# Two transformer blocks in fp32 on one core: a new order for the seven products of the second MLP matrix, with the embedding parts, the row transposes and a bank moved with it

## The chip, the cores and the metric

The kernel is one program on one core of a Trainium2 chip. The metric is device time in microseconds (us) of one execution, taken as the median of several. Shown here are three executions and, apart from them, one execution recorded by the hardware profiler.

The engines are TensorE (PE: matmuls and transposes), VectorE (DVE), ScalarE (ACT), GpSimd (POOL) and SyncE (SP, which here only issues transfers). Each works through its own list of instructions in order; an instruction that needs another engine's result waits on a semaphore, and everything behind it on its engine waits too.

## The reference, cut to what matters

512 tokens of width 1024 pass through two blocks. `first_block` has an RWKV-7 time mix and differential attention, `second_block` a gated linear attention and a dilated attention. Behind the mixing, both blocks do the same three things, and the change lies there:

```
merged = g_a * (o_a @ w_proj_a) + g_b * (o_b @ w_proj_b)
x = x + merged @ w_out                                    # the out projection ("wo")
h = rmsnorm(x)
x = x + square(relu(h @ w_ff1)) @ w_ff2                   # the MLP: 1024 -> 4096 -> 1024
gate = sigmoid(rmsnorm(x) @ w_ple_gate)
x = x + (p @ w_ple) * gate                                # the embedding part: p is 512 x 256
```

`second_block` spells them `w_mlp1`, `w_mlp2`, `w_pp` and `w_pg`, and ends in a last rmsnorm. Everything is fp32.

## The kernel before, in words

**Numbers.** A product of two fp32 matrices is made of three products of rounded parts: high by high, low by high and high by low. ACT makes the high part of a tile (a copy that rounds: `wh` of a weight, `SH`, `XH`, `YH`... of an activation), DVE the low part (tile minus high part: `wl`, `SL`, `XL`, `YL`...). A weight tile of 128 x 1024 is a unit; three slots each for `wh` and `wl` go round. In the trace all matmuls are line 131, transposes line 134, ACT operations mostly line 141, DVE's line 155 (two tensors) or 163 (with a scale). A matmul with 512 columns is the usual one.

**The MLP.** The 4096 hidden columns are worked through in four groups g of 1024. For each group the first matrix gives eight tiles `f1` (g, n), n = 0..7; ACT applies relu (tile T) and square (tile `hid`). The second matrix is multiplied with seven products in place of eight (Strassen's way, in Winograd's form): the group's activations and weights are cut into quarters, and some operands are sums of quarters. The activation sums are made on DVE, in place over `hid` and in a tile `E` (`dv_operands`: events ss 1 to 4). The weight sums are made on DVE in the four quarter tiles RB 11, 12, 21, 22 (`dv_weight_sums`: ts 1 to 4), which SP loads anew for each group (`sp_second`), each load waiting until the last low part was taken from the tile. Each product i (`product`) needs `SH` and `SL` of its operand (two slots) and two weight units, has 24 matmuls in two PSUM banks, and DVE then adds the two banks into `xt` with the reciprocal norm (`dv_mlp`).

**Who stands between.** In groups 0 to 2 the products alternate with the f1 tiles of the next group: f1(g+1, 0), product 0, f1(g+1, 1), product 1, and so on. In the last group there are no further f1 tiles. The embedding product `p @ w_ple` (two parts of 24 matmuls, `ple`) stands between the products there. The `prows` tile holds p by rows; PE transposes it (`pe_ple`, eight 128 x 128 transposes), and ACT and DVE split the result into `PPH` and `PPL`. As the last quarters of `xt` are complete, PE transposes them (`pe_turn`, in the order TURN, into banks 6 and 7), DVE adds them to XT (block 0), and the gate product begins on `YA`, `YB` (the first block's normed input, in halves), with its mean square taken by PE as ones x ACC.

**Order.** Each engine's instruction list comes out of a planner. The code of one kind of work on one engine is a lane; `arrange` plays all lanes against a clock of its own. On PE the lanes have fixed ranks, with the dense products (`pe_dense`) last but with patience before others come between. On DVE and ACT, lanes with no fixed slack (low parts, high parts, operands, weight sums) are ranked by when PE is to need them. So an edit in one lane moves others' instructions as well.

**Banks.** `self.ring` is the list of PSUM banks that the dense tiles take in turn (`take_bank`): (0, 1) in the MLP, (0, 1, 2) behind it.

Of the kernel before, what the change touches and what calls it, by code (L numbers as in the profile page):

```python
# [227 lines left out]
class Kernel:  # L228
# [273 lines left out]
    def pe_dense(self, s):  # L502
# [31 lines left out]
        for n in range(3, 8):  # L534
            yield from self.fm(s, "Y", ("pg", n))
        yield from self.fm_pair(s, "X2", ("ha",), ("gqk", 0, 0))
# [5 lines left out]
        yield from self.tm(s, "X2", ("gv", 0), [("xm", 0, 3, 7)])  # L542
# [24 lines left out]
    def dense_mlp(self, s, blk, merged, x):  # L567
# [1205 lines left out]
    def plan_ff(self, blk, w1, wp):  # L1773
        for j in range(4):
            self.plan("f1", w1, 0, 8, 256 * j, 256, "n", 2)
        made = ((11, "rb", 11), (21, "rb", 21), (11, "ts", 1), (11, "ts", 2), (22, "rb", 22), (12, "ts", 3), (21, "ts", 4))
# [5 lines left out]
        for g in range(3):  # L1782
            for n in range(8):
                if n % 2 == 0:
                    ci = self.chunk(w1, 0, 8, 1024 * (g + 1) + 128 * n, 256)
                self.piece(ci, "n", 2, n % 2)
                if n < 7:
                    product(g, n)
        for i in range(7):
            product(3, i)  # L1790
            if i == 2:
                ci = self.chunk(wp, 0, 2, 0, 1024)
            if i in (2, 5):
                self.piece(ci, "n", 2, i == 5)
# [78 lines left out]
    def mlp_tiles(self):  # L1873
# [21 lines left out]
        for blk in range(2):  # L1895
            for g in range(4):
# [13 lines left out]
    PRODUCTS = (("M1", (2, 3), True, 0, 0, 1), ("M2", (6, 7), True, 0, 0, 1), ("M5", (4, 5), True, 1, 1, 1), ("M6", (2, 3), False, 0, 1, -1),  # L1910
                ("M3", (4, 5), False, 0, 1, 1), ("M7", (2, 3), False, 1, 1, -1), ("M4", (2, 3), False, 1, 0, 1))
# [4 lines left out]
    def operand(self, g, i):  # L1916

        q = self.quarter
        return (q(g, 0, 0), q(g, 0, 1), self.E[:, :, :], q(g, 0, 0), q(g, 0, 1), q(g, 1, 0), q(g, 1, 1))[i]

    def operand_made(self, blk, g, i):
        tiles = {0: range(4), 1: range(4, 8), 6: range(4, 8)}.get(i)
        if tiles:
            return [self.at("hid", blk, g, n) for n in tiles]
        return [self.at("ss", blk, g, {2: 1, 3: 2, 4: 4, 5: 3}[i])]
# [11 lines left out]
    def dv_operands(self, s):  # L1937
        dv, at = self.dv, self.at
        for blk in range(2):
            for g in range(4):  # L1940
# [9 lines left out]
                self.splitting = x0 + 2  # L1950
# [7 lines left out]
                self.splitting = x0 + 3  # L1958
# [12 lines left out]
    def dv_weight_sums(self, s):  # L1971

        dv, at, RB = self.dv, self.at, self.RB
        for blk in range(2):
            for g in range(4):
                part = lambda q, h: RB[q][:, 2 * h:2 * h + 2, :]
                u = self.f2_units[blk, g]
                for k, q, a, b, i, lows, loads in ((1, 11, 11, 12, 2, 0, (11, 12)), (3, 12, 12, 22, 5, None, (22,)), (2, 11, 11, 22, 3, 2, ()), (4, 21, 11, 21, 6, 1, (21,))):
# [22 lines left out]
    def dv_mlp(self, s, blk):  # L2001
        dv = self.dv
        for (b, g, i), x in self.slot.items():
# [3 lines left out]
            for j in range(2):  # L2007
# [4 lines left out]
                if blk == 0 and g == 0 and i in (0, 2, 3, 6):  # L2012
# [30 lines left out]
    TURN = ((11, 1), (12, 4), (22, 5), (21, 6))  # L2043
    TURNED = (4, 5, 6, 7, 0, 1, 2, 3)

    def pe_turn(self, s, blk):
        pe = self.pe
        free = {p: ("f2e", blk, 3, 1, p) for p in range(2)}
        for q, i in self.TURN:
            th, nh = q // 10 - 1, q % 10 - 1  # L2050
            for p in range(2):
                yield
                pe.wait_ge(*[self.at("f2e", blk, 3, i, j) for j in range(2)], self.at(*free[p]))
# [5 lines left out]
                free[p] = ("fte", blk, q, p)  # L2059
# [13 lines left out]
    def ac_turn(self, s, gain):  # L2073
        ac = self.ac
        for q, i in self.TURN:
            th, nh = q // 10 - 1, q % 10 - 1
            for p in range(2):
                for f in range(2):
                    n = 4 * nh + 2 * p + f
                    yield  # L2080
                    ac.wait_ge(self.at("ft", 1, q, p), *([self.at("sl", 1, 3, 3), self.at("ss", 1, 3, 4)] if n < 4 else []))
                    ac.copy(self.YH[n][:, 256 * th:256 * th + 256], self.ps[6 + p][:, 256 * f:256 * f + 256], self.vec(gain, n)).then_inc(*s.up(("h", "Y2", n, th)))

    def dv_turn2(self, s, gain):
        dv = self.dv
        for q, i in self.TURN:
            th, nh = q // 10 - 1, q % 10 - 1
            for p in range(2):
                for f in range(2):
                    n, ts = 4 * nh + 2 * p + f, slice(256 * th, 256 * th + 256)  # L2090
                    yield
                    dv.wait_ge(self.at("h", "Y2", 4 * nh + 2 * p + 1, th), *([self.at("sl", 1, 3, 4)] if n < 4 else []))
# [3 lines left out]
    def ac_mlp3(self, s, gain):  # L2096
        ac = self.ac
        for n in self.TURNED:
            yield
            ac.wait_ge(self.at("xm", 0, 3, n))  # L2100
            ac.copy(self.YH[n], self.XT[:, n, :], self.vec(gain, n)).then_inc(*s.up(("h", "Y", n)))
            yield
# [4 lines left out]
    def dv_mlp3(self, s, gain):  # L2107
        dv = self.dv
        for n in self.TURNED:
# [3 lines left out]
            if n != 4:  # L2113
                yield
                dv.wait_ge(self.at("ysqd", n), s.now())
                dv.tensor_tensor(self.ACC[:, :], self.ACC[:, :], self.tile["ysq", n][:, :], ALU.add).then_inc(*s.up(("ysa", n)))
# [71 lines left out]
    def pe_norms(self, s):  # L2188
# [5 lines left out]
        yield from self.pe_mean_squares(s, "rst1", self.ACC, self.ps[4], ("ysa", 3), ("ysqd", 4), ("f2e", 0, 3, 4, 0))  # L2194
        yield from self.pe_spread(s, "rst1", self.T[2], self.ps[4], ("ms1",))
        yield from self.pe_mean_squares(s, "m1", self.ACC, self.ps[4], ("sqp", 7), ("rst1",))
        yield from self.pe_mean_squares(s, "m2", self.ACC2, self.ps[5], ("sqp2", 7), ("f2e", 0, 3, 4, 1))
# [732 lines left out]
    def pl_lnf(self, s):  # L2930
        pl = self.pl
        yield
        pl.wait_ge(self.at("sl", 1, 3, 2), self.at("ss", 1, 3, 2))
# [27 lines left out]
    SQUARED = [(0, 0), (1, 0), (0, 1), (1, 1), (2, 1), (3, 1), (2, 0), (3, 0)]  # L2961

    def ac_last_squares(self, s):
        ac = self.ac
        for x, (j, nh) in enumerate(self.SQUARED):
            sq = self.tile["lsq", x]
            yield
            ac.wait_ge(self.at("f2e", 1, 3, (1, 4, 5, 6)[x // 2], j % 2), *self.freed("lsq", x))
# [299 lines left out]
```

## Time and profile before

| | |
|---|---|
| median of three executions | 1932.8 us (1928.93, 1932.8, 1934.3) |
| profiled execution, own time | 1934.82 us |
| its span, first to last instruction | 1933.0 us |
| mean granted clock of TensorE | 0.989 of full |
| busy time of PE, DVE | 1883.5 us (97%), 1151.1 us (60%) |
| busy time of ACT, POOL | 855.3 us (44%), 98.8 us (5%) |
| chain of work that ended last, by engine | PE 87%, DVE 7%, ACT 2%, DMA 2%, issue 2% |

The last row follows the work back from the last instruction, at each step to what released it. A busy share says how much of the span an engine had work, not whether anyone waited for it. The granted clock is the share of full TensorE speed (2.4 GHz) that was granted; 0.50 is the lower level of 1.2 GHz.

### The profile page before, as it was taken

What the parts mean: (1) busy time and instruction counts of PE and PEld (TensorE: products, weight loads), DVE (VectorE), ACT (ScalarE), POOL (GpSimd) and SP (SyncE); (2) the same over time, 40 slices, a digit from 0 to 9 for tenths busy, and PEclk for the clock granted to TensorE, in tenths of its full rate; (3) what the DMA queues carried; (4) which work ended last, traced back from release to release, by engine and by line L of the source; (5) the groups of instructions that cost most, each with busy time, mean ns of one, the idle gap of its engine ahead of it and who ended that gap; (6) DMA issues with size and microseconds to landing.
All of it is one profiled execution on the core that took longest, in us unless ns stands there. A gap on an engine that the chain in (4) does not pass through costs nothing.

```text
span 1933.0 us, 23466 instructions
## 1 busy us (share of the span) xinstructions
PE 1883.5 (97%) x9426; PEld 1551.5 (80%) x9426; DVE 1151.1 (60%) x1777; ACT 855.3 (44%) x1318; POOL 98.8 (5%) x153
## 2 busy tenths in 40 slices
PE   7999999998999999899999999999999999999897
PEld 5887778877788888778888888898887888888786
DVE  5769665446456857788734335424345456857775
ACT  6435554323344444456634324333233444445363
POOL 2110111002000000000100000000000000000000
PEclk9999999999999999899999999999999999999999
DMA  6233211129423232212431222232255223232211
GB/s 226 66 91 119 85 55 40 45 78 328 127 66 110 87 131 87 87 44 79 142 117 47 88 69 85 92 105 82 93 196 185 87 66 122 81 124 89 97 44 65
DMA packets 158175, 194.65 MB, mean 101 GB/s; under 512 B 14826, under 2 KB 118932, under 8 KB 158067
## 3 DMA queue, kind: packets, MB, share of 16 engines
q1 hardware_dynamic: 151954, 181.91, 29.2%
q0 software_dynamic: 4528, 8.94, 1.4%
q10 hardware_dynamic: 1584, 2.30, 0.3%
q8 instruction: 75, 1.23, 0.3%
q14 instruction: 34, 0.27, 0.0%
HBM read 179.41 MB, written 15.54 MB: 101 GB/s over the span
## 4 chain that ended last, share of the span: by engine, by line
PE 87%; DVE 7%; ACT 2%; DMA 2%; issue 2%; POOL 0%; POOLq 0%; DVEq 0%; SPq 0%; ACTq 0%
PE bank L131 84%; PE bank L134 3%; DVE wl L155 1%; DMA prows<-in_p_dram 1%; ACT L141 1%; ACT wh L141 1%; DVE ACC L155 1%; DVE T L155 1%; DVE RB L155 0%; DMA scr_x<-XT 0%; DVE XL L163 0%; DVE XT L155 0%; ACT GP L141 0%; DVE ML L155 0%; DVE xt L163 0%
## 5 line engine op out<-in xcount | busy, mean ns | idle before, releaser
L131 PE MATMUL bank<-XH,wh 128*128 128x512 f32 (+1 forms) x1272 | 504.1, 396 | 5.3 <-DVE XL L163 2.2
L131 PE MATMUL bank<-XL,wh 128*128 128x512 f32 (+1 forms) x1272 | 497.0, 391 | 1.0 <-DVE XL L163 1.0
L141 ACT ACTIVATE wh<-raw 128x1024 fp32r<-128x1024 f32 (+1 forms) x239 | 252.8, 1058 | 534.2 <-PE bank L131 526.2
L155 DVE TENSOR_TENSOR wl<-raw,wh 128x1024 fp32r<-128x1024 f32 x238 | 292.8, 1231 | 269.6 <-ACT wh L141 269.1
L131 PE MATMUL bank<-XH,wl 128*128 128x512 f32 x1264 | 318.7, 394 | 0.0
L131 PEld LDWEIGHTS bank<-XH,wh 128*128 128x128 f32 (+1 forms) x1272 | 238.8, 188 | 60.5 <-issue 2.6
L131 PEld LDWEIGHTS bank<-XL,wh 128*128 128x128 f32 (+1 forms) x1272 | 238.9, 188 | 51.0 <-DVE XL L163 2.4
L131 PEld LDWEIGHTS bank<-XH,wl 128*128 128x128 f32 x1264 | 236.3, 189 | 49.6 <-issue 0.6
L141 ACT ACTIVATE wh<-RB 128x1024 fp32r<-128x1024 f32 x112 | 119.1, 1063 | 158.6 <-PE bank L131 158.6
L155 DVE TENSOR_TENSOR wl<-RB,wh 128x1024 fp32r<-128x1024 f32 x112 | 137.0, 1223 | 76.5 <-ACT wh L141 76.4
L131 PE MATMUL bank<-wh,SL 128*128 128x512 f32 x448 | 140.2, 395 | 12.6 <-DVE SL L155 12.6
L131 PE MATMUL bank<-wh,SH 128*128 128x512 f32 x448 | 139.6, 393 | 0.0
L131 PE MATMUL bank<-wl,SH 128*128 128x512 f32 x448 | 139.3, 392 | 0.0
L131 PEld LDWEIGHTS bank<-wh,SL 128*128 128x128 f32 x448 | 85.2, 191 | 31.1 <-DVE SL L155 13.5
L131 PEld LDWEIGHTS bank<-wl,SH 128*128 128x128 f32 x448 | 85.2, 190 | 18.0
L131 PEld LDWEIGHTS bank<-wh,SH 128*128 128x128 f32 x448 | 84.6, 190 | 17.6
L163 DVE SCALAR_TENSOR_TENSOR xt<-bank,scales,xt 128x512 f32<-128x512 f32 x104 | 77.7, 747 | 4.1 <-DVE xt L163 0.9
L155 DVE TENSOR_TENSOR RB<-RB,RB 128x1024 f32<-128x1024 f32 x64 | 78.2, 1221 | 1.4
L155 DVE TENSOR_TENSOR T<-bank,RST 128x512 f32<-128x512 f32 x58 | 40.0, 689 | 60.6 <-PE bank L131 60.3
L131 PE MATMUL bank<-wh,XH 128*128 128x512 f32 x192 | 60.4, 396 | 0.0
L131 PE MATMUL bank<-wh,XL 128*128 128x512 f32 x192 | 59.7, 392 | 0.0
L131 PE MATMUL bank<-wl,XH 128*128 128x512 f32 x192 | 59.7, 392 | 0.0
(446 smaller groups left out, 2583.7 us busy)
## 6 DMA issues: line engine op xcount, KB each, us to landing
raw<-in_w_in_dram SPq DMA_DIRECT2D x58, 1024.0 KB, 5.2
RB<-in_w_ff_dram SPq DMA_DIRECT2D x16, 1024.0 KB, 5.0
raw<-in_w_ff_dram SPq DMA_DIRECT2D x16, 1024.0 KB, 5.3
RB<-in_w_mlp_dram SPq DMA_DIRECT2D x16, 1024.0 KB, 5.1
raw<-in_w_mlp_dram SPq DMA_DIRECT2D x16, 1024.0 KB, 5.3
raw<-in_w_out_dram SPq DMA_DIRECT2D x8, 1024.0 KB, 5.2
scr_x<-XT POOLq DMA_DIRECT2D x16, 256.0 KB, 4.6
XT<-scr_x SPq DMA_DIRECT2D x8, 512.0 KB, 10.9
```

The source lines that it names most:

```text
L131: return self.put(ns, lambda e: e.matmul(out, lhsT, rhs, start=start, stop=stop, skip_group_check=True))
L134: return self.put(109, lambda e: e.transpose(out, in_, ident))
L141: return self.put(ns, lambda e: e.activation(out, in_, func, bias=bias, scale=scale), func)
L155: return self.put(self.ns(out), lambda e: e.tensor_tensor(out, a, b, op))
L163: return self.put(self.ns(out), lambda e: e.scalar_tensor_tensor(out, a, s, b, op0, op1))
```

## The change

- **Order of the products.** Before: M1, M2, M5, M6, M3, M7, M4. After: M1, M5, M6, M3, M7, M2, M4. The bank pairs follow: (2, 3) and (4, 5) in turn, where M2 had (6, 7). The operand sums, the weight sums, the loads of the quarters and the transposes of finished quarters follow that order; the last weight sum goes into RB 12.
- **Embedding parts.** In the last group the two `ple` parts stand ahead of product 0 and of product 1. Before, they stood behind product 2 and behind product 5.
- **Row transposes.** `pe_ple` additionally waits for the last tile of the out projection.
- **Bank.** In block 0 the ring has a fourth bank (3) from the MLP to the start of the second block's projections.
- **Squares.** For the gate's norm in block 0 the squares on ACT come behind each four copies, and DVE's additions into ACC behind each four low parts.

```diff
-    PRODUCTS = (("M1", (2, 3), True, 0, 0, 1), ("M2", (6, 7), True, 0, 0, 1), ("M5", (4, 5), True, 1, 1, 1), ("M6", (2, 3), False, 0, 1, -1),
-                ("M3", (4, 5), False, 0, 1, 1), ("M7", (2, 3), False, 1, 1, -1), ("M4", (2, 3), False, 1, 0, 1))
+    PRODUCTS = (("M1", (2, 3), True, 0, 0, 1), ("M5", (4, 5), True, 1, 1, 1), ("M6", (2, 3), False, 0, 1, -1), ("M3", (4, 5), False, 0, 1, 1),
+                ("M7", (2, 3), False, 1, 1, -1), ("M2", (4, 5), True, 0, 0, 1), ("M4", (2, 3), False, 1, 0, 1))
...
         for i in range(7):
+            if i < 2:
+                yield from self.ple(s, blk, i)
             yield from self.product(s, blk, 3, i)
-            if i in (2, 5):
-                yield from self.ple(s, blk, i == 5)
-        self.ring, self.last_use[2] = (0, 1, 2), self.pair_after[2]
+        self.ring, self.last_use[2], self.last_use[3] = (0, 1, 2) if blk else (0, 1, 2, 3), self.pair_after[2], self.pair_after[3]
...
-        made = ((11, "rb", 11), (21, "rb", 21), (11, "ts", 1), (11, "ts", 2), (22, "rb", 22), (12, "ts", 3), (21, "ts", 4))
+        made = ((11, "rb", 11), (11, "ts", 1), (11, "ts", 2), (22, "rb", 22), (12, "ts", 3), (21, "rb", 21), (12, "ts", 4))
...
-                yield
-                low(1)
-                yield
-                self.splitting = x0 + 4
-                dv.wait_ge(s.now(), at("sh", blk, g, 1))
-                dv.tensor_tensor(q(g, 0, 1), q(g, 0, 1), q(g, 0, 0), ALU.add).then_inc(*s.up(("ss", blk, g, 4)))
-                for i in range(2, 7):
+                for i in range(1, 7):
                     yield
                     low(i)
+                    if i == 2:
+                        yield
+                        self.splitting = x0 + 3
+                        dv.wait_ge(s.now(), at("sh", blk, g, 2))
+                        dv.tensor_tensor(q(g, 0, 0), q(g, 0, 1), q(g, 0, 0), ALU.add).then_inc(*s.up(("ss", blk, g, 4)))
...
-                for q in (11, 22, 12, 21):
+                for q in (22, 11, 21, 12):
                     yield
                     if g:
                         u = self.f2_units[blk, g - 1]
-                        sp.wait_ge(at("lo", u[{11: 3, 22: 4, 12: 5, 21: 6}[q]][1]), *{11: [at("ts", blk, g - 1, 4, 1)], 22: [at("ts", blk, g - 1, 2, 1)], 12: [], 21: []}[q])
+                        sp.wait_ge(at("lo", u[{11: 2, 22: 3, 12: 6, 21: 5}[q]][1]), *{11: [at("ts", blk, g - 1, 4, 1)], 22: [at("ts", blk, g - 1, 3, 1)], 12: [], 21: [at("ts", blk, g - 1, 4, 1)]}[q])
...
-    TURN = ((11, 1), (12, 4), (22, 5), (21, 6))
+    TURN = ((12, 3), (22, 4), (11, 5), (21, 6))
...
-            pe.wait_ge(self.at("prw", blk))
+            pe.wait_ge(self.at("prw", blk), self.at("acc", "wo", blk, 7))
```

The rows below are the instruction lists as the two programs have them, buffer numbers included. The first place is PE in block 0's out projection (`MH`, `ML`: high and low part of the merged rows). Before:

```order
L131 MATMUL bank<-MH_203,wl_77 128x512 x6
L131 MATMUL bank<-MH_203,wl_75 128x512 x6
L134 MATMUL bank<-ident_49,prows_226 128x128 x8
L131 MATMUL bank<-MH_203,wh_74 128x512
L131 MATMUL bank<-ML_204,wh_74 128x512
```

After, at the end of the projection, where the first f1 tile (`XH`, `XL`) follows:

```order
L131 MATMUL bank<-MH_203,wh_72 128x512
L131 MATMUL bank<-ML_204,wh_72 128x512
L131 MATMUL bank<-MH_203,wl_75 128x512 x8
L134 MATMUL bank<-ident_49,prows_226 128x128 x8
L131 MATMUL bank<-XH_67,wh_73 128x512
L131 MATMUL bank<-XL_68,wh_73 128x512
```

The eight transposes move from the middle of the projection's eight tiles to behind the last one. The second place is DVE at the last group of block 0, from the moment at which `hid` is complete. Before:

```order
L155 TENSOR_TENSOR E_216<-hid_206 128x1024
L155 TENSOR_TENSOR hid_206<-hid_206 128x4x256
L155 TENSOR_TENSOR wl_75<-RB_214,wh_72 128x1024
L163 SCALAR_TENSOR_TENSOR xt_207<-bank,scales_228,xt_207 128x512
L155 TENSOR_TENSOR wl_76<-RB_212,wh_73 128x1024
L163 SCALAR_TENSOR_TENSOR xt_207<-bank,scales_228,xt_207 128x512
L155 TENSOR_TENSOR RB_212<-RB_212,RB_215 128x1024
L155 TENSOR_TENSOR hid_206<-E_216,hid_206 128x4x256
L155 TENSOR_TENSOR SL_210<-hid_206,SH_208 128x1024
```

After:

```order
L155 TENSOR_TENSOR E_216<-hid_206 128x1024
L155 TENSOR_TENSOR hid_206<-hid_206 128x4x256
L155 TENSOR_TENSOR hid_206<-E_216,hid_206 128x4x256
L155 TENSOR_TENSOR wl_75<-raw_71,wh_72 128x1024
L155 TENSOR_TENSOR SL_210<-E_216,SH_208 128x1024
L155 TENSOR_TENSOR wl_76<-RB_212,wh_73 128x1024
```

The low part that product 1 needs stood ninth, and now stands fifth, and it is of `E`, no longer of a `hid` quarter. The third place is PE at the end of block 0's MLP, where the last products (`wl_75` by `SH`), the last quarter's transposes and the gate product (`YA`, `YB`) meet. Before:

```order
L131 MATMUL bank<-wl_75,SH_209 128x512 x2
L134 MATMUL bank<-ident_49,xt_207 128x128 x8
L131 MATMUL bank<-YA_217,wh_73 128x512
...
L131 MATMUL bank<-YA_217,wl_75 128x512 x4
L131 MATMUL bank<-ones_52,ACC_61 128x1 x4
L131 MATMUL bank<-YB_219,wh_73 128x512
```

After:

```order
L131 MATMUL bank<-YA_217,wl_76 128x512 x4
L134 MATMUL bank<-ident_49,xt_207 128x128 x8
L131 MATMUL bank<-YA_217,wh_74 128x512
...
L131 MATMUL bank<-YA_217,wl_75 128x512 x4
L131 MATMUL bank<-YB_219,wh_73 128x512
...
L131 MATMUL bank<-YB_219,wl_75 128x512 x4
L131 MATMUL bank<-ones_52,ACC_61 128x1 x4
```

Before, the transposes stood ahead of the gate product and the mean square (ones x ACC) behind 36 matmuls of it. Now the transposes stand behind the first 12 matmuls, and the mean square behind 72. The transposes that spread its result over the tokens follow 12 matmuls later before, and 16 matmuls later now.

## Rows read from the trace of the kernel before

**Rows 1.** Waits of PE by what ended them: total, times, longest
```profile
PE bank L131 <- DVE SL L155: 12.6, 2, 6.3
PE bank L134 <- DMA prows<-in_p_dram: 8.2, 2, 5.3
PE bank L131 <- DVE XT L155: 1.6, 2, 0.8
```

**Rows 2.** PE's timeline, row transposes of block 0: start, duration, instruction, [idle before]
```profile
472.13 1.97 PE L134 MATMUL bank<-ident,prows 128*128 128x128 f32 x8 [5.31 <-DMA prows<-in_p_dram]
473.75 0.78 PE L131 MATMUL bank<-MH,wh 128*128 128x512 f32 x1
...
477.31 0.40 PE L131 MATMUL bank<-MH,wh 128*128 128x512 f32 x1
```

**Rows 3.** PE's timeline, row transposes of block 1
```profile
1484.33 1.97 PE L134 MATMUL bank<-ident,prows 128*128 128x128 f32 x8 [2.92 <-DMA prows<-in_p_dram]
1485.95 0.78 PE L131 MATMUL bank<-OGH,wh 128*128 128x512 f32 x1
...
1488.20 0.39 PE L131 MATMUL bank<-OGH,wh 128*128 128x512 f32 x1
```

**Rows 4.** PE's timeline, end of block 0's out projection
```profile
510.93 1.98 PE L131 MATMUL bank<-MH,wl 128*128 128x512 f32 x8
513.68 0.50 PE L131 MATMUL bank<-XH,wh 128*128 128x512 f32 x1 [0.78 <-DVE XT L155]
```

**Rows 5.** PE's timeline, last group: product 1 of block 0, then of block 1
```profile
816.03 1.22 PE L131 MATMUL bank<-wh,SL 128*128 128x512 f32 x2 [6.32 <-DVE SL L155]
...
822.12 0.62 PE L131 MATMUL bank<-wl,SH 128*128 128x512 f32 x2
...
1829.02 1.22 PE L131 MATMUL bank<-wh,SL 128*128 128x512 f32 x2 [6.32 <-DVE SL L155]
...
1832.51 0.63 PE L131 MATMUL bank<-wl,SH 128*128 128x512 f32 x2
```

**Rows 6.** Stretches: length, busy time of PE, PEld, DVE, ACT, POOL, granted clock, DMA share, GB/s
```profile
472.13:477.31 5.18, 5.18 (x17) 4.41 (x17) 2.07 (x4) 1.81 (x3) 0.00 (x0) 0.50 1.04 372
803.66:867.74 64.08, 56.09 (x250) 45.42 (x248) 54.34 (x58) 33.77 (x41) 0.00 (x0) 0.92 0.08 25
1816.65:1879.47 62.82, 56.23 (x256) 45.84 (x254) 52.16 (x59) 38.55 (x62) 0.55 (x1) 0.95 0.10 33
882.49:921.35 38.86, 38.56 (x170) 30.39 (x168) 36.30 (x57) 26.71 (x42) 1.05 (x2) 1.00 0.36 109
```

**Rows 7.** DVE's timeline, last group of block 0
```profile
806.51 1.22 DVE L155 TENSOR_TENSOR E<-hid 128x1024 f32<-128x1024 f32 x1
...
814.76 1.22 DVE L155 TENSOR_TENSOR SL<-hid,SH 128x1024 fp32r<-128x1024 f32 x1
```

**Rows 8.** PE's timeline, last quarter's transposes, block 0 and block 1
```profile
866.92 1.06 PE L134 MATMUL bank<-ident,xt 128*128 128x128 f32 x8 [1.67 <-DVE xt L163]
867.74 2.09 PE L131 MATMUL bank<-YA,wh 128*128 128x512 f32 x8
...
1878.57 1.06 PE L134 MATMUL bank<-ident,xt 128*128 128x128 f32 x8 [0.27 <-DVE xt L163]
```

**Rows 9.** PE's, then DVE's timeline, norm of block 0's gate and its first eviction
```profile
876.30 1.05 PE L131 MATMUL bank<-ones,ACC 128*128 128x1 f32 x8
...
882.49 0.69 DVE L155 TENSOR_TENSOR T<-bank,RST 128x512 f32<-128x512 f32 x1
```

**Rows 10.** DVE's, then PE's timeline, start of the second block's projections
```profile
920.60 0.75 DVE L163 SCALAR_TENSOR_TENSOR XL<-XT,gg,XH 128x512 fp32r<-128x512 f32 x1 [0.79 <-ACT XH L141]
...
921.41 0.44 PE L131 MATMUL bank<-XL,wh 128*48 128x512 f32 x1 [0.36 <-DVE XL L163]
```

**Rows 11.** SP's, then ACT's timeline: load of a chunk of the first MLP matrix, first use
```profile
751.90 0.37 SPq L119 DMA_DIRECT2D raw<-in_w_ff_dram  x1
...
782.10 1.06 ACT L141 ACTIVATE wh<-raw 128x1024 fp32r<-128x1024 f32 x1 [3.43 <-PE bank L131]
```

More of the change, by code:

```diff
@@ L541, in pe_dense @@
                         yield from self.fm(s, "X2", ("gqk", c, 2 * pr + i))
-        yield from self.tm(s, "X2", ("gv", 0), [("xm", 0, 3, 7)])
+        yield from self.tm(s, "X2", ("gv", 0), self.last_use[3])
         yield from self.tm(s, "X2", ("gv", 1), [("free", "gv", 0, 3)])
@@ L1788, in plan_ff @@
                     product(g, n)
+        ci = self.chunk(wp, 0, 2, 0, 1024)
         for i in range(7):
+            if i < 2:
+                self.piece(ci, "n", 2, i)
             product(3, i)
[L1791 to L1794, printed above, removed]
     def sp_spill1(self, s):
@@ L1918, in operand @@
         q = self.quarter
-        return (q(g, 0, 0), q(g, 0, 1), self.E[:, :, :], q(g, 0, 0), q(g, 0, 1), q(g, 1, 0), q(g, 1, 1))[i]
+        return (q(g, 0, 0), self.E[:, :, :], q(g, 0, 0), q(g, 0, 0), q(g, 1, 0), q(g, 0, 1), q(g, 1, 1))[i]
     def operand_made(self, blk, g, i):
-        tiles = {0: range(4), 1: range(4, 8), 6: range(4, 8)}.get(i)
+        tiles = {0: range(4), 5: range(4, 8), 6: range(4, 8)}.get(i)
         if tiles:
             return [self.at("hid", blk, g, n) for n in tiles]
-        return [self.at("ss", blk, g, {2: 1, 3: 2, 4: 4, 5: 3}[i])]
+        return [self.at("ss", blk, g, {1: 1, 2: 2, 3: 4, 4: 3}[i])]
     def ac_operands(self, s):
@@ L1977, in dv_weight_sums @@
                 u = self.f2_units[blk, g]
-                for k, q, a, b, i, lows, loads in ((1, 11, 11, 12, 2, 0, (11, 12)), (3, 12, 12, 22, 5, None, (22,)), (2, 11, 11, 22, 3, 2, ()), (4, 21, 11, 21, 6, 1, (21,))):
+                for k, q, a, b, i, lows, loads in ((1, 11, 11, 12, 1, 0, (11, 12)), (2, 11, 11, 22, 2, 1, (22,)), (3, 12, 12, 22, 4, None, ()), (4, 12, 11, 21, 6, 4, (21,))):
                     for h in range(2):
@@ L2011, in dv_mlp @@
                 dv.wait_ge(self.at("f2", blk, g, i, j), self.at("irst", blk))
-                if blk == 0 and g == 0 and i in (0, 2, 3, 6):
+                if blk == 0 and g == 0 and i in (0, 1, 2, 6):
                     dv.tensor_scalar(acc, self.ps[pair[j]][:, :], by, ALU.mult).then_inc(*s.up(("f2e", blk, g, i, j)))
@@ L2047, in pe_turn @@
         pe = self.pe
-        free = {p: ("f2e", blk, 3, 1, p) for p in range(2)}
+        free = {p: self.FF_FREE[blk] for p in range(2)}
         for q, i in self.TURN:
@@ L2052, in pe_turn @@
                 yield
-                pe.wait_ge(*[self.at("f2e", blk, 3, i, j) for j in range(2)], self.at(*free[p]))
+                pe.wait_ge(*[self.at("f2e", blk, 3, i, j) for j in range(2)], *[self.at(*e) for e in free[p]])
                 for f in range(2):
@@ L2058, in pe_turn @@
                 t.then_inc(*s.up(("ft", blk, q, p)))
-                free[p] = ("fte", blk, q, p)
+                free[p] = [("fte", blk, q, p)]
     def dv_turn(self, s):
@@ L2101, in ac_mlp3, with ac_squares @@
             ac.copy(self.YH[n], self.XT[:, n, :], self.vec(gain, n)).then_inc(*s.up(("h", "Y", n)))
+            if n in (7, 3):
+                yield from self.ac_squares(s, n - 3)
+    def ac_squares(self, s, n0):
+        ac = self.ac
+        for n in range(n0, n0 + 4):
             yield
@@ L2112, in dv_mlp3 @@
             dv.scalar_tensor_tensor(self.YL[n], self.XT[:, n, :], self.vec(gain, n), self.YH[n].bitcast(F32), ALU.mult, ALU.subtract).then_inc(*s.up(("l", "Y", n)))
-            if n != 4:
+            for m in {7: (5, 6, 7), 3: (0, 1, 2, 3)}.get(n, ()):
                 yield
-                dv.wait_ge(self.at("ysqd", n), s.now())
-                dv.tensor_tensor(self.ACC[:, :], self.ACC[:, :], self.tile["ysq", n][:, :], ALU.add).then_inc(*s.up(("ysa", n)))
+                dv.wait_ge(self.at("ysqd", m), s.now(), *([self.at("ysqd", 4)] if m == 5 else []))
+                dv.tensor_tensor(self.ACC[:, :], self.ACC[:, :], self.tile["ysq", m][:, :], ALU.add).then_inc(*s.up(("ysa", m)))
     def pl_ple(self, s, blk, p):
@@ L2193, in pe_norms @@
         yield from self.pe_turn(s, 0)
[L2194 removed]
+        yield from self.pe_mean_squares(s, "rst1", self.ACC, self.ps[4], ("ysa", 3), ("ysqd", 4), ("f2e", 0, 3, 5, 0))
         yield from self.pe_spread(s, "rst1", self.T[2], self.ps[4], ("ms1",))
         yield from self.pe_mean_squares(s, "m1", self.ACC, self.ps[4], ("sqp", 7), ("rst1",))
[L2197 removed]
+        yield from self.pe_mean_squares(s, "m2", self.ACC2, self.ps[5], ("sqp2", 7), ("f2e", 0, 3, 5, 1))
         yield from self.pe_spread(s, "rstB", self.T[2], self.ps[4], ("m1",))
```

17 lines of the change are left out of this document (9 added, 8 removed).

## The prediction

> **What bounds the kernel now.** PE does: it is busy 97% of the span and holds 87% of the chain that ended last, so a gain can only come out of its remaining idle time or out of stretches in which it runs at a lower clock. I therefore read the list of PE's waits first. It has two large entries beyond the start-up, and both are at places that the change touches: the low part `SL`, twice, 12.6 us together, and the rows of p, twice, 8.2 us together [rows 1]. Then I read PE's timeline around each, because a long wait has a second price. Behind the 5.31 us wait for `prows` the granted clock is 0.50, the lower level of 1.2 GHz, until 477.31 [rows 2, 6], and the same shape stands behind each `SL` wait. Full speed is 0.227 us for a 512-column matmul: eight have a record of 1.98 us, which is seven steps and a last 0.39 [rows 4]. In the slow stretches one step is about 0.43. Between the end of one matmul's slot and the next start there is 0.16 us more than the idle figure, since the record of the last one runs on (513.68 less 510.93 and eight steps is 0.94, the row says 0.78) [rows 4].
>
> **Part 1, row transposes.** Block 0: the wait is 5.31 + 0.16 = 5.47 us, the eight transposes take 473.75 - 472.13 = 1.62, and the eight matmuls up to 477.31 take 3.56 where 8 x 0.227 = 1.81 would do [rows 2]. Together 5.47 + 1.62 + 1.75 = 8.8. Block 1: 2.92 + 0.16, 1.62, and six matmuls up to 1488.20 in 2.25 instead of 1.36 [rows 3]: 3.1 + 1.6 + 0.9 = 5.6. In the new place the load has had some 35 us more, so nothing waits for it. The transposes themselves are not removed. But there PE already stands idle for 0.94 us, for the first normed tile [rows 4] (in block 1 too: two waits, 1.6 us together [rows 1]), and eight transposes at full clock take 867.74 - 866.92 = 0.82 us [rows 8]. They fit, so I charge 0.1 per block: **8.7 + 5.5 gained**. If that cover were gone, they would cost 0.8 each. `PPH` and `PPL` are made later, but the first user is the last group, hundreds of us on.
>
> The Trainium skill (TensorE: Matmul & The Clock Gate, Part 4: PE-mode transpose) gives about 275 ns for one such transpose inside a kernel. Eight one after the other would be 2.2 us by that, an estimate, and would overrun the gap by 1.3 us per block, 2.6 in all. The row's spacing of 0.10 us each speaks against it here, and the sum goes by the row.
>
> **Part 2, the last group.** Before, product 1 (M2) follows product 0 at once and needs hidden tiles that were just made. `E` starts at 806.51, when the last `hid` is there, and DVE then has three weight low parts, two evictions and a weight sum ahead of the `SL` at 814.76 [rows 7]. PE waits 6.32 + 0.16 = 6.48 us. The following 14 matmuls, up to 822.12, take 6.09 instead of 3.18, so 2.91 more. In block 1 the wait is the same 6.48, and eight slow matmuls take 3.49 instead of 1.81, 1.68 more [rows 5]. The last quarter's transposes wait 1.67 + 0.16 = 1.83 and 0.27 + 0.16 = 0.43 us for `xt` [rows 8]. At stake are 6.48 + 2.91 + 1.83 = **11.2** in block 0 and 6.48 + 1.68 + 0.43 = **8.6** in block 1.
>
> After, embedding part 0, product 0 and embedding part 1 stand between the last f1 tile and product 1. Each is 24 matmuls, 5.44 us, so product 1 begins at 803.66 + 16.3 = 820.0 in the old trace's time. The `SL` that it needs is that of `E`, now the fifth instruction after `hid` is complete: 806.51 + 5 x 1.22 = 812.6 at the latest. It has 7 us to spare, and this wait goes away. What is left is DVE's volume. In the 64.08 us from 803.66 to the gate product DVE is busy 54.34 us [rows 6]. Take out 11.2 and 52.9 us are left for the same work: DVE is 1.4 us over. What is late then is the last eviction into `xt`. Although the transposes that need it now stand 12 matmuls (2.7 us) into the gate product, I place 1.4 us there and 0.3 at quarter 11, whose product comes just before. In block 1, 62.82 - 8.6 = 54.2 us stand against 52.16 of DVE work [rows 6]. It fits on average, but DVE's evictions and the low parts of the next operand `YA`/`YL` bunch at the end; I take 1.3, a little less than in block 0, with 0 and 3 as ends. Gain: 11.2 - 1.7 = **9.5**, and 8.6 - 1.3 = **7.3**.
>
> **Part 3, the gate of block 0.** The mean square stands 36 matmuls later on PE and its spread 4 more: 40 x 0.227 = 9.1 us. The first eviction was 882.49 - 867.74 = 14.75 us after the gate product's start Y0 [rows 8, 9]. One weight low part (1.1 us) stood just before it and need not now, so it comes at 14.75 + 9.1 = 23.8 or 22.7; I take 23.2. The gate product has a fourth bank, so PE can run on meanwhile. But DVE's evictions, additions and low parts start later as well, and at their end the second block's projections wait for the last `XL`. From the first eviction to the end of that `XL` (920.60 + 0.75) are 38.86 us, of which DVE is busy 36.30 [rows 6, 10]. Two weight low parts (2.3 us) move ahead of it, and 34.0 to 36.6 are left; with a backlog the idle part shrinks, so I take 34.5. The last `XL` is then there at Y0 + 57.7. PE waited only 0.36 for it [rows 10], so it was due at Y0 + 53.3, and at 54.1 with the last quarter's transposes now inside. That makes a wait of 3.6, less the old 0.36: **3.2 lost**. Ends: 0, if the evictions start at 22.7 and the idle is gone and ACT's hand-offs shrink too; 8, with 23.8 + 36.6 (a wait of 6.3) and the lower clock behind it, which was worth 1.7 to 2.9 above. The bank itself brings nothing by itself, as PE has no wait for a bank in that stretch.
>
> **Part 4, the steady groups.** In groups 0 to 2 an f1 tile (5.44 us) stands between any two products, so the slack of product 1's operand is that of the new last group, 7 us. No PE wait of these groups is in the list before, so there is nothing to gain. I charge nothing; the cover is the f1 tiles.
>
> **Sum.** 8.7 + 5.5 + 9.5 + 7.3 - 3.2 = 27.8. Span 1933.0 becomes 1905.2, the execution's own time 1934.8 becomes 1907.0. That execution was 2.0 above the median of 1932.8, so the median becomes 1905.0.
>
> **Rivals.** *A, nothing given back:* all 34.0 us at stake (8.7 + 5.5 + 11.2 + 8.6) arrive and the gate costs nothing. For it: ACT and DVE are played against one clock by the planner, which may move YL work out of the way. Against it: DVE at 1.4 over. Time 1932.8 - 34.0 = 1898.8. *B, DVE becomes the bound of the last groups and the gate:* the gate wait is 8, and each last group gives back 3 more. Gain 27.8 - 4.8 - 6 = 17, time 1915.8. For it: 54.34 us of work in 52.9. *C, only the row transposes pay:* the `SL` wait turns into one of like size later in the group, for an operand sum or a weight sum. Gain 14.2 - 3.2 = 11, time 1921.8. Against it: the 7 us of slack. *D, slower:* in the six steady groups the operand of product 1 comes late, because `hid`'s three sums now stand in front of weight low parts and evictions that PE needs sooner. Each miss would be priced like the old one, up to 6.5 us plus 2.9 of clock, six times 56 us: 1961. It decides once a group loses 27.8 / 6 = 4.6 us, which needs the operand some 11 us later than I place it. The same rival could come from SP. The reload of a quarter now waits for the last weight sum, in front of the next weight chunk in SP's list. But that chunk is issued at 751.90, lands in about 5 us and is first used at 782.10 [rows 11], so a delay under 25 us is free.
>
> **Chances.** Forecast (gain 23 to 31) 0.60, A 0.15, B 0.15, C 0.06, no net gain 0.02, D 0.02. A measurement tells a change of 0.3%, 5.8 us, from none: faster 0.96, same 0.02, slower 0.02. The forecast's own range is 1902 to 1910. The full range goes from A, less 2 for the spread of the runs, to B: 1897 to 1916. Outside it are C, D, no gain, and the edges of A and B, some 0.15.
>
> **What would show it.** In the new trace PE's list should have no `prows` and no `SL` entry, and the transposes of `prows` should stand at about 505 without a slow stretch behind them. There should be a wait for `xt` of about 1 to 2 us at the last quarter of each block, and one of 3 to 4 us for `XL` or `XH` at the start of the second block's projections. The stretch from the last f1 tile to the gate product should shrink from 64.1 to about 54.5. The prediction is wrong if a wait of over 3 us stands in a steady group, if the transposes cost 2 us at their new place, or if the gate's last `XL` is on time or over 6 us late.

## The result and the profile after

The changed kernel takes 1908.9 us in the median (1906.97 to 1911.25, four runs) against 1933.4 us for the kernel before (four executions, one more than in the table above). The ratio is 0.9878, with a 95% interval of 0.9859 to 0.9898: 24.5 us faster. Timed twice more beside the experiments it gave 1907.2 and 1907.1 us, where the kernel before gave 1932.0 and 1931.9: 24.8 us faster both times. The profiled execution has a span of 1905.0 us and took 1906.97 us itself. The forecast was a gain of 27.8 us, which made 1905 for the median and 1905.2 for the span. The span came out at that, the medians' gain is 3 us smaller.

The page's head, of the changed kernel:

```profile
span 1905.0 us, 23473 instructions
PE 1876.2 (98%) x9426; PEld 1547.3 (81%) x9426; DVE 1148.1 (60%) x1777; ACT 853.9 (45%) x1318; POOL 99.7 (5%) x153
```

PE's waits in it, by what ended them (total, times, longest):

```profile
PE bank L131 <- DVE XL L163: 4.1, 2, 2.2
...
PE bank L131 <- ACT XH L141: 1.4, 1, 1.4
PE bank L131 <- ACT T L141: 1.1, 4, 0.3
PE bank L134 <- DVE xt L163: 1.1, 1, 1.1
...
PE bank L134 <- DVE YA L163: 0.6, 1, 0.6
```

Both large entries of [rows 1] are gone, `SL` and `prows`. New are `XH`, a larger share for `XL`, two more waits for `T`, and one for `YA`. Next PE's timeline at the new place of the row transposes (two rows), in embedding part 0, at the last quarter's transposes of block 0, at the start of the second block's projections, and at the transposes of quarter 11 in block 1's last group:

```profile
500.29 1.06 PE L134 MATMUL bank<-ident,prows 128*128 128x128 f32 x8
501.11 0.47 PE L131 MATMUL bank<-XH,wh 128*128 128x512 f32 x1
...
794.70 0.50 PE L131 MATMUL bank<-PPH,wh 128*128 128x512 f32 x1 [0.28 <-ACT T L141]
...
849.92 1.07 PE L134 MATMUL bank<-ident,xt 128*128 128x128 f32 x8 [1.07 <-DVE xt L163]
...
902.01 0.43 PE L131 MATMUL bank<-XH,wh 128*48 128x512 f32 x1 [1.37 <-ACT XH L141]
904.38 0.43 PE L131 MATMUL bank<-XL,wh 128*48 128x512 f32 x1 [1.95 <-DVE XL L163]
...
1845.41 0.63 PE L134 MATMUL bank<-ident,xt 128*128 128x128 f32 x4 [0.60 <-DVE YA L163]
```

The transposes take 501.11 - 500.29 = 0.82 us, in the time in which PE stood idle before [rows 4]; the first f1 tile follows them with no wait. The wait for `xt` is 1.07 + 0.16 us (the 0.16 is the prediction's: the time that the record before a wait runs on). The two waits at the start of the projections are 1.37 + 1.95 + 0.32 = 3.64 us.

To see where the time went I cut PE's timeline at seven instructions that every version has, and took differences of their starts. They are the `X,UB` matmuls that wait for `X` (at about 258 us), the first wait for `T` in each block's f1 tiles, the end of the last f1 tile in each block, the `KI` transposes that PE waits for (about 957), and the first instruction behind the transposes of block 1's last quarter. All numbers are us.

| stretch | before | changed | difference | forecast |
|---|---|---|---|---|
| start to `X,UB` | 259.9 | 258.0 | -1.9 | none |
| to f1 of block 0: row transposes | 266.2 | 257.4 | -8.8 | -8.7 |
| f1 and the steady groups, block 0 | 277.6 | 277.6 | 0.0 | 0 |
| last group, gate, start of block 1 | 168.7 | 164.1 | -4.6 | -6.3 |
| to f1 of block 1: row transposes | 566.7 | 561.2 | -5.5 | -5.5 |
| f1 and the steady groups, block 1 | 277.6 | 277.6 | 0.0 | 0 |
| last group, block 1 | 62.8 | 55.5 | -7.2 | -7.3 |
| to the end | 53.6 | 53.6 | 0.0 | 0 |

Behind the start, two more executions of the changed kernel give the same stretches within 0.1 us, but for the second stretch of one of them (258.0). The first row is no effect of the change, as experiment 5 shows; without it the traces differ by 26.1 us. The kernel before has one trace only, so what chance did in it shows only where an experiment runs the same instructions again.

### The profile page after: what moved, and what is told of

Its sections match the earlier page's. It is cut to its first block, busy times and chain, and to the rows that moved or that the text cites. A ratio compares the mean times of both kernels' runs of the same rounds, so it can differ in the third digit from the quotient of the medians.

```text
span 1905.0 us, 23473 instructions
## 1 busy us (share of the span) xinstructions
PE 1876.2 (98%) x9426; PEld 1547.3 (81%) x9426; DVE 1148.1 (60%) x1777; ACT 853.9 (45%) x1318; POOL 99.7 (5%) x153
## 3 DMA queue, kind: packets, MB, share of 16 engines
q8 instruction: 75, 1.23, 0.3%
## 4 chain that ended last, share of the span: by engine, by line
PE 88%; DVE 7%; ACT 2%; issue 2%; DMA 1%; POOL 0%; POOLq 0%; DVEq 0%; ACTq 0%
PE bank L131 86%; PE bank L134 2%; DVE wl L155 2%; DVE xt L163 1%; ACT L141 1%; DVE XL L163 1%; DVE T L155 0%; DMA scr_x<-XT 0%; DVE XT L155 0%; DVE RB L155 0%; ACT wh L141 0%; DVE ACC L155 0%; ACT GP L141 0%; DVE SL L155 0%; DVE YA L163 0%
```

## The experiments

Below, *gate* is the fourth row of the table above (before 168.7, changed 164.1) and *last 1* its row for block 1's last group (62.8 and 55.5). Both are lengths in us.

**1. Row transposes back in the projection.**

```diff
-            pe.wait_ge(self.at("prw", blk), self.at("acc", "wo", blk, 7))
+            pe.wait_ge(self.at("prw", blk))
```

> The changed kernel with one part undone: the row transposes may go as soon as the rows of p have landed, so they stand in the middle of the out projection again. Theory of the sum (5.47 + 1.62 + 1.75 and 3.1 + 1.6 + 0.9 us, less the 0.94 us gap that they fill now): both waits for prows come back, 5.3 and 2.9 us, with the lower clock behind them, and the kernel is 14 us slower than the changed one, 10 faster than before. Rival: the transposes cost as much at their new place as they did at the old one (they delay the first f1 tile), so the difference is under 6 us.

1920.6 us, ratio 0.9943 (0.9928 to 0.9958): 11.7 to 13.5 slower than the changed kernel, by which of its medians is taken. PE's timeline of this version, both blocks:

```profile
468.51 1.97 PE L134 MATMUL bank<-ident,prows 128*128 128x128 f32 x8 [4.90 <-DMA prows<-in_p_dram]
...
1474.83 1.85 PE L134 MATMUL bank<-ident,prows 128*128 128x128 f32 x8 [2.78 <-DMA prows<-in_p_dram]
```

The two stretches are 264.7 and 566.6 us, 7.3 and 5.4 above the changed kernel's, 12.7 together where 14.3 separate the kernels at the top. The waits are shorter by 0.4 and 0.1 us here; the rest of the difference is in the slow matmuls behind, of which there are fewer in block 0. The rival, a cost at the new place, is out: all other stretches stay.

**2. Only the embedding parts first**, in the kernel before (`plan_ff` moved with it, as in the change):

```diff
         for i in range(7):
+            if i < 2:
+                yield from self.ple(s, blk, i)
             yield from self.product(s, blk, 3, i)
-            if i in (2, 5):
-                yield from self.ple(s, blk, i == 5)
```

> The kernel before with one part done: the embedding parts ahead of product 0 and product 1 in the last group, old order of the products. Theory 1, it is the two embedding parts (10.9 us of PE work) that give DVE the time: the SL of product 1 is there at about 804 of the changed kernel's time against 810 needed, no SL wait, and the kernel gains 15 to 18 us of its own, 1916. Rival, the new order of the products is what removes the wait, since M5 needs E where M2 needs a later low part: the wait for SL stays above 3 us in both blocks and the gain is under 10 us.

1921.2 us, ratio 0.9943 (0.9927 to 0.9960): 10.6 us faster than the kernel before, where 15 to 18 were expected. No wait for `SL` is left. Gate 162.5, last 1 56.3: 6.2 and 6.5 us gained. The mechanism is as theory 1 has it; its size was set too high, since I counted the 18 us at stake and not what is given back at the end of the group.

**3. The new order without the embedding parts in front**: the changed kernel with the same lines the other way round. The moved row transposes, the bank and the squares stay in.

> The changed kernel with one part undone: the embedding parts behind products 2 and 5 again, new order of the products. Theory 1 (see the run with the embedding parts alone): E is begun at the same moment, and the SL of product 1 stands tenth on DVE behind it, some 10 us, where product 0 covers 3; a wait of about 7 us comes back in both blocks with the lower clock behind it, and the kernel is 15 to 19 us slower than the changed one. Rival: the order alone shortens the chain to the SL, the wait is under 3.5 us and the clock stays up, 3 to 8 us slower.

1918.8 us, ratio 0.9931 (0.9917 to 0.9946), 10 to 12 slower than the changed kernel. PE's timeline, product 1 in both blocks:

```profile
807.65 1.22 PE L131 MATMUL bank<-wh,SL 128*128 128x512 f32 x2 [7.03 <-DVE SL L155]
...
1813.04 1.22 PE L131 MATMUL bank<-wh,SL 128*128 128x512 f32 x2 [7.03 <-DVE SL L155]
```

The wait is back at 7.03 us, longer than the old 6.32 [rows 5]. Last 1 is 64.2, worse than before by 1.4; gate is 166.6. The new order does not bring the low part any earlier by itself. Again the sum was put too high (15 to 19 expected), for the same reason. Against the kernel before, the order, the bank and the squares together gain 2.1 us in gate and lose 1.4 in last 1: 0.7 us in all without the embedding parts. The rest of this version's 13.0 us is the moved row transposes.

**4. Both parts that pay, alone**: the kernel before with the edits of 1 (forward) and 2, old order, three banks, squares one by one. Run twice, the second time beside the changed kernel.

> The kernel before with two parts done: embedding parts ahead of products 0 and 1, row transposes behind the projection; old order of the products, three banks, squares one by one. Theory 1, from the runs so far: these two parts hold the whole gain and the new order of the products adds nothing; adding up the stretches gives the changed kernel's time less 1.6 us at block 0's gate and plus 0.7 us in block 1's last group, so 1 us faster, and within 2.5 us of it in any case. Rival, the parts need each other (the order of the products pays only once the embedding parts stand first): 5 us or more slower than the changed kernel.

> The kernel before with embedding parts first and rows behind the projection alone, timed in five rounds beside the changed kernel. From the stretches of its first trace: 1.8 us (0.09%) faster than the changed kernel; by the medians the two can hardly be told apart, and neither is 3 us apart from the other. Rival: the old order of the products costs 3 us or more.

1905.8 us, ratio 0.9870 (0.9854 to 0.9887), then 1906.6 us, 0.9873 (0.9858 to 0.9888). Gate is 161.5 and 163.1, last 1 is 56.3 both times. So the whole of what is left out is worth 0.8 us in block 1's last group, and costs 1.0 to 2.6 in block 0. The version has two of the change's parts and is as fast as the whole of it; the medians can't tell them apart. PE's timeline of the first run, last quarter of block 0, then the second block's projections:

```profile
847.28 0.95 PE L134 MATMUL bank<-ident,xt 128*128 128x128 f32 x7 [1.32 <-DVE xt L163]
851.55 1.11 PE L131 MATMUL bank<-YA,wh 128*128 128x512 f32 x2 [2.05 <-DVE YA L163]
...
904.72 0.44 PE L131 MATMUL bank<-XL,wh 128*48 128x512 f32 x1 [0.35 <-DVE XL L163]
```

The 3.64 us wait is down to 0.35 + 0.16, and 3.7 us of waits stand at the gate product's start instead. The clock stays up behind the short wait at the projections, where the changed kernel loses 3.2 us to the lower one (worked out in part 3 below). The second run has the same waits within 0.02 us, and yet its gate is 1.5 us longer. The stretch behind the 2.05 us wait shows why, in the second run:

```profile
852.20:856.20 4.00, 3.59 (x8) 2.67 (x9) 3.69 (x7) 3.36 (x7) 0.00 (x0) 0.59 0.00 0
```

In the first run the clock of the same stretch (852.20 to 856.20) is 1.00.

**5. The changed kernel itself, again**, twice.

> The changed kernel itself, on the same chip as the three runs beside it: 1906 to 1911 us. Theory on the start: which of two courses the first 60 us take (a slow stretch behind the wait for LD at 37 to 38 us, or none) is settled anew in each execution, as the instruction lists there are the same in all kernels; so this execution may well have it, and would then end 1.5 to 2 us later than the first one profiled. Rival: the course belongs to the kernel, and it comes without the slow stretch again.

> The changed kernel itself, five rounds beside the run above: 1906 to 1909 us, a ratio of 0.987 to 0.988 to before. Every stretch behind the first 260 us as in the two traces of it so far, within 0.1 us; only the start differs, by up to 2.5 us.

1907.2 us, ratio 0.9875 (0.9861 to 0.9890), and 1907.1 us, 0.9871 (0.9857 to 0.9886). In the first of them `X,UB` starts at 259.4, in the second at 257.5, with the same lists. PE's timeline of the first, and stretches of it (length, busy times, granted clock third from the end):

```profile
37.91 0.47 PE L131 MATMUL bank<-LD,LS 128*128 128x512 f32 x1 [1.48 <-ACT LD L141]
```
```profile
36.00:38.00 2.00, 0.52 (x3) 0.12 (x2) 1.78 (x3) 1.93 (x4) 0.00 (x0) 1.00 0.00 0
38.00:40.00 2.00, 2.00 (x5) 1.01 (x6) 0.00 (x0) 1.99 (x4) 0.00 (x0) 0.92 0.00 0
40.00:42.00 2.00, 2.00 (x6) 1.52 (x6) 1.73 (x2) 2.00 (x4) 0.00 (x0) 0.50 0.01 4
```

The first execution of the changed kernel had 0.40 us at this place and a clock of 1.00 from 36 to 46 us. Its slow stretch came earlier. These are 8 to 24 us in the first execution of the changed kernel, then in this one:

```profile
8.00:24.00 16.00, 13.11 (x57) 10.77 (x57) 10.54 (x17) 13.02 (x22) 6.61 (x12) 0.89 0.83 244
```
```profile
8.00:24.00 16.00, 12.20 (x61) 9.26 (x59) 11.25 (x23) 13.47 (x23) 7.20 (x13) 1.00 0.83 248
```

The kernel before went the way of this one (1.00 from 8 to 24 us, 0.72 from 40 to 46). The course of the start belongs to the execution, and with it the 1.9 us of the first table.

**6. Squares one by one**, in the changed kernel:

```diff
             ac.copy(self.YH[n], self.XT[:, n, :], self.vec(gain, n)).then_inc(*s.up(("h", "Y", n)))
-            if n in (7, 3):
-                yield from self.ac_squares(s, n - 3)
+            yield
+            ac.wait_ge(self.at("imb", 0), *(self.freed("ysq", n) if n != 4 else []))
...
```

> The changed kernel with one part undone: squares and their additions follow each single tile, so the mean square stands behind 36 matmuls of the gate product again, and the last quarter's transposes stand ahead of it. Theory, the late mean square makes the 3.3 us wait at the second block's projections: that wait falls under 1 us, and a wait for xt of 1 to 3 us at the transposes remains or grows, since nothing of the gate product stands before them; 1 to 3 us faster than the changed kernel in all. Rival, DVE's volume makes the wait wherever the mean square stands: the 3.3 us stay within 0.7, and the kernel is no faster or up to 3 us slower.

1906.3 us, ratio 0.9868 (0.9854 to 0.9883); gate 163.7, 0.4 less. Both halves of the theory came about, and cancel. PE's timeline, and the clock behind the first of its rows:

```profile
849.93 1.07 PE L134 MATMUL bank<-ident,xt 128*128 128x128 f32 x8 [3.78 <-DVE xt L163]
...
905.64 0.43 PE L131 MATMUL bank<-XL,wh 128*48 128x512 f32 x1 [0.35 <-DVE XL L163]
```
```profile
850.75:854.75 4.00, 4.00 (x14) 3.14 (x13) 3.90 (x7) 2.67 (x5) 1.05 (x2) 0.57 0.00 0
```

The last `xt` comes at the same moment as in the changed kernel (849.93 and 849.92), whatever PE does meanwhile. The wait for it, 3.78 us, is longer than the 1 to 3 expected, and the lower clock stands behind it.

**7. Three banks for the gate**, in the changed kernel:

```diff
-        self.ring, self.last_use[2], self.last_use[3] = (0, 1, 2) if blk else (0, 1, 2, 3), self.pair_after[2], self.pair_after[3]
+        self.ring, self.last_use[2], self.last_use[3] = (0, 1, 2), self.pair_after[2], self.pair_after[3]
```

> The changed kernel with one part undone: three banks for the gate of block 0. With the first eviction at about 23 us after the gate product's start and 5.4 us of matmuls per tile, three banks are full after 16 us. Theory: PE then waits for a bank, 3 to 7 us, and about as much of the 3.3 us wait at the second block's projections goes away; 1 to 5 us slower in all. Rival, as the prediction has it: the bank brings nothing by itself, within 1 us.

1908.3 us, ratio 0.9883 (0.9866 to 0.9899); gate 164.7, 0.6 more. PE's timeline:

```profile
868.13 1.12 PE L134 MATMUL bank<-ident,T 128*128 128x128 f32 x4 [2.99 <-DVE T L166]
870.73 1.65 PE L131 MATMUL bank<-YB,wh 128*128 128x512 f32 x3 [1.48 <-DVE T L155]
...
907.93 0.43 PE L131 MATMUL bank<-XL,wh 128*48 128x512 f32 x1 [0.35 <-DVE XL L163]
```

The fourth bank moves a wait of 4.5 us from the gate to the end of the stretch and saves 0.6. Without it the part up to the `ones` x `ACC` matmuls of the projections (at 904.99 in the changed kernel) is 3.8 us longer, and the part behind them 3.2 us shorter, as the lower clock behind the projections' wait is gone. "Brings nothing by itself" was near in size, though for another reason than I gave: without it PE does wait.

**8. Product 0 ahead of both embedding parts**, in the changed kernel:

```diff
         for i in range(7):
-            if i < 2:
-                yield from self.ple(s, blk, i)
             yield from self.product(s, blk, 3, i)
+            if i == 0:
+                yield from self.ple(s, blk, 0)
+                yield from self.ple(s, blk, 1)
```

> The changed kernel with one place moved: product 0, then both embedding parts, then product 1. The 0.28 us wait for T in the second bank of embedding part 0 (0.44 with the tail, in both blocks) goes away, since product 0 stands between; the slack of product 1's SL is the same. Theory: 0.5 to 1 us faster by the stretch from the last f1 tile to the gate product, too little for the medians. Rival: product 0's own low part or weights come late without the embedding part in front, a wait of over 1 us for SL, wl or SH, and slower.

1907.1 us, ratio 0.9874 (0.9859 to 0.9889). The wait for `T` is gone and one of 0.34 us for `PLT` between the two parts stands in its place, so last 1 stays at 55.5. Neither theory had that one. Gate is 165.2, 1.1 more, and all of it lies behind the projections' last wait. From 904 to 916, in steps of 4 us, the clock is 0.57, 0.50 and 0.65 there, so the slow stretch is longer in this execution.

**9. Less work for DVE**, in the changed kernel. The six additions of the turned quarters 12, 22 and 11 to XT take 64 columns instead of 512, so this version leaves most of block 0's MLP result out:

```diff
-                dv.tensor_tensor(o, o, self.ps[6 + p][:, :].rearrange("p (f t) -> p f t", f=2), ALU.add).then_inc(
+                c = 256 if q == 21 else 32
+                dv.tensor_tensor(o[:, :, 0:c], o[:, :, 0:c], self.ps[6 + p][:, :].rearrange("p (f t) -> p f t", f=2)[:, :, 0:c], ALU.add).then_inc(
```

> The changed kernel with DVE's work at the end of block 0's last group cut: the six additions of the turned quarters 12, 22 and 11 to XT take 64 columns in place of 512, so most of the MLP's result stays out of XT in block 0. That frees some 3 us of DVE ahead of the last eviction into xt. Theory, DVE's volume sets the last quarter and the gate: the 1.07 us wait for xt goes, the mean square comes earlier, and the 3.3 us wait at the second block's projections shrinks by about the same 3 us; 3 to 6 us faster than the changed kernel, with the lower clock gone there as well. Rival, the waits come from PE's banks and the order, not from DVE's time: under 1 us faster.

1900.5 us, ratio 0.9841 (0.9824 to 0.9857), 6.6 us faster than the changed kernel; gate 156.4, that is 7.7 less. No wait for `xt` is left in block 0, and one wait at the projections:

```profile
899.78 0.43 PE L131 MATMUL bank<-XL,wh 128*48 128x512 f32 x1 [0.70 <-DVE XL L163]
```

About 3 us of DVE work taken away give back 7.7 us, more than the 3 to 6 expected. The traces add it up: the waits for `XT` and `xt` in the last group are gone (0.46 and 1.23 us), the wait at the projections is 0.86 in place of 3.64, and the same instructions from `ones` x `ACC` to the `KI` transposes take 3.2 us less, at full clock:

```profile
900.38:949.16 48.78, 47.35 (x224) 39.18 (x224) 40.64 (x61) 36.20 (x49) 7.43 (x11) 1.00 0.41 137
```

This is the clearest sign that DVE's volume sets block 0's last group and gate. The planner also moved the mean square forward here, from behind 72 matmuls of the gate product to behind 60, so part of it may be order; no run separates the two.

## Why the prediction held, step by step

**Part 1, row transposes: right to 0.1 us** (8.8 and 5.5 measured, 8.7 and 5.5 forecast). The price of such a wait is three things, and all three had to be counted: the wait, the transposes at the lower clock, and the slow matmuls behind. The transposes fit into the idle gap before the f1 tile. That it came to 0.1 us is partly luck, since the number of slow matmuls differs between executions: with the transposes at the old place the stretch was longer by 8.8, 8.3 and 7.3 us in block 0 (before, experiments 2 and 1) and by 5.5, 6.6 and 5.4 in block 1. The group of the last group's transposes in the kernel before, by line (busy, mean ns of one, idle before):

```profile
L134 PE MATMUL bank<-ident,xt 128*128 128x128 f32 x32 | 4.2, 275 | 1.7 <-DVE xt L163 1.7
```

One record is 275 ns long, which is what the Trainium skill states for a transpose within a kernel (TensorE: Matmul & The Clock Gate, Part 4: PE-mode transpose). But eight start 0.10 us apart and take 0.82 us, so the figure is the length of one and not the price of one more. The estimate of 2.2 us for eight, worked out from it, did not come.

**Part 2, the last groups: right in mechanism.** The `SL` of product 1 was ready 7 us early, as worked out. DVE's timeline of the changed kernel, with the `SL` at its end (needed by PE at 810.41):

```profile
796.67 1.22 DVE L155 TENSOR_TENSOR E<-hid 128x1024 f32<-128x1024 f32 x1
...
801.46 1.22 DVE L155 TENSOR_TENSOR SL<-E,SH 128x1024 fp32r<-128x1024 f32 x1
```

Block 1 gained 7.2 where 7.3 was forecast, but the last part of that sum is right by luck. I had given 1.3 us back at its end, where DVE's work bunches, and looked for a wait for `xt` at the last quarter. That wait did not come. One for `YA` at quarter 11, one quarter earlier (0.60 + 0.16), and the one for `T` named below (0.44) came in its place, and add up to 1.2. In block 0 the wait at the last quarter was 1.23 against 1.4, and one for `XT` at quarter 22 took 0.30 + 0.16. I missed a wait in both blocks, for `T` in the second bank of embedding part 0 (0.28 + 0.16): with two banks in the ring, the part that now follows f1 at once needs the bank that ACT is still emptying. And DVE's own timeline shows why the last `xt` is late:

```profile
844.15 1.41 DVE L163 SCALAR_TENSOR_TENSOR YA<-XT,pvt,YA 128x512 fp32r<-128x512 f32 x2
845.48 1.22 DVE L155 TENSOR_TENSOR wl<-raw,wh 128x1024 fp32r<-128x1024 f32 x1
846.62 0.75 DVE L163 SCALAR_TENSOR_TENSOR YA<-XT,pvt,YA 128x512 fp32r<-128x512 f32 x1
847.28 0.75 DVE L163 SCALAR_TENSOR_TENSOR xt<-bank,scales,xt 128x512 f32<-128x512 f32 x1
```

It is busy without a gap, with the gate product's low parts ahead of the eviction. DVE is busy 55.6 us of the 57.8 from the last f1 tile to the end of those transposes:

```profile
792.90:850.74 57.84, 56.20 (x261) 45.53 (x260) 55.64 (x60) 32.67 (x40) 0.00 (x0) 1.00 0.11 36
```

The prediction counted the embedding parts and the order as one thing. Experiments 2, 3 and 4 show that the embedding parts carry the gain, and that the new order has no share in it that a median could show.

**Part 3, the gate: right in place, its cost a quarter too low** (3.2 forecast, 4.4 measured). The first eviction came at 870.38, 24.5 us after the gate product's first matmul (845.92), where 23.2 was forecast, and the last `XL` ended 58.4 us after it (57.7). PE would have needed it 54.8 us after it (54.1), so both ends came 0.7 us later than placed and their difference, the wait, was 3.64 us (3.6). Its size is right in part by luck. The mis-sized term is the clock behind this wait, which I had put into the range's end and not into the value. Here are the 8 us from 902.75, with most of the second wait in them:

```profile
902.75:906.75 4.00, 2.20 (x10) 1.88 (x10) 2.78 (x4) 1.40 (x2) 0.00 (x0) 0.79 0.46 121
906.75:910.75 4.00, 4.00 (x15) 3.52 (x15) 2.04 (x5) 0.00 (x0) 1.63 (x2) 0.50 0.41 143
```

The lower clock holds for some 7 us, in the kernel before for some 3.5. These are the same instructions in both, from `ones` x `ACC` to the `KI` transposes, before and changed:

```profile
922.01:972.40 50.39, 48.95 (x223) 40.35 (x223) 40.65 (x61) 36.24 (x49) 7.46 (x11) 0.97 0.37 123
```
```profile
904.99:957.00 52.01, 50.57 (x223) 41.94 (x224) 40.73 (x61) 36.20 (x49) 7.43 (x11) 0.93 0.40 132
```

At full clock they take 48.8 us (experiments 2, 4, 7 and 9). So the clock cost 3.2 us in the changed kernel, in all three of its traces, and 1.6 in the trace before: 1.6 more. Block 0's part as a whole gained 4.6 and not 6.3. Of the missing 1.7, some 0.5 lies in the last group (`T` and `XT`) and 1.2 in the gate: the 1.6 of clock, less 0.4 gained elsewhere in it.

**Part 4, the steady groups: right.** 277.6 us before and after, in both blocks, in every version.

**Rivals.** A (all 34.0 us) is out by the waits at the last quarter and the gate; B has the right mechanism, a DVE that is busy nearly throughout, but of its 10.8 us beyond the forecast only 1.7 came; C and D did not occur. The medians moved by 24.5 to 24.8 and not by 26.1. The start can make that difference, and so can the 1.6 us of lower clock in the one trace before, which four of the six traces with the same last wait of 0.35 us there did not have; which of the two it is was not separated.

## What to carry to other kernels

- When a change has several parts, add up the waits by stretch and then run the parts alone. Here two small moves (independent work between an operand's inputs and its use, and a transfer's user moved past its landing) hold the whole gain, and the larger rewrite of the order holds none that the medians show.
- A wait on the busiest engine that is filled with work costs nothing there, but look for who is saturated next. With DVE at 96% of a stretch, undoing a mean square's place or a bank only moved waits of 3 to 4.5 us from one end to the other; taking 3 us of work off DVE gave 7.7, of which 3.2 was clock.
- The length of a stretch mostly repeated to 0.1 us from trace to trace, where whole executions spread by 4 us. Where the clock fell differently, two traces of the same instructions differed by 1.0 to 1.6 us; and two traces were 0.6 and 0.7 us longer in the second stretch at full clock. So judge parts of a few us by stretches, with the granted clock beside them.

## What the runs showed of the hardware

- The same instruction list takes one of two courses in its first 46 us. In ten of the thirteen traces the clock was 0.89 from 8 to 24 us and 1.00 from 40 to 46, and `X,UB` started at 256.8 to 259.3; in three (before, experiment 3 and the second of the changed kernel) it was 1.00 and then 0.72 to 0.74, and `X,UB` started at 259.4 to 259.9. The wait for `LD` on PE was between 0.40 and 1.70 us where there was one. That is up to 3.1 us of an execution.
- The clock behind a short wait is not settled by the wait. Behind 4.9 to 7.0 us in the middle of the kernel it was at the lower level each time, behind 3.78 us 0.57, and behind the 2.8 and 2.9 us for `prows` in block 1 the next matmuls started 0.43 us apart too. Behind waits of 1.32 and 2.05 us near each other it stayed at 1.00 in one execution and was 0.59 in another of the same kernel, which is the 1.5 us between their gates. Behind a last wait of 0.35 us at the projections the instructions up to the `KI` transposes took 48.8 us in four traces (experiments 2 and 7, both of 4) and 50.4 in two (before and experiment 6); with the 1.37 and 1.95 us there they took 52.0 in every trace of the changed kernel.
